# The root of one norm moved from the transposed rows into the values' copies and the means under the head norms

## The reference, cut to what matters

```python
h = h + sq_relu_mlp(rmsnorm(h, norm_mlp[0]), w_up[0], w_down[0])     # end of layer 0
kv = rmsnorm(h, kv_norm) @ w_kv                                      # (256, 512)
k_shared = rmsnorm(kv[..., :256].reshape(B, S, 4, 64), k_norm)       # norm of each head
v_shared = kv[..., 256:].reshape(B, S, 4, 64)
proj = rmsnorm(h, norm_mix[1]) @ w_in[1]                             # (256, 1024)
q = rmsnorm(proj[..., :768].reshape(B, S, 12, 64), q_norm)
mqh = rmsnorm(proj[..., 768:].reshape(B, S, 4, 64), mem_q_norm[1])
main_out = swa_sink_attention(q, k_shared, v_shared, sinks)
mem_out = memory_attention(mqh, mk, mv)
h = h + concatenate([main_out, mem_out]) @ w_out[1]
# rmsnorm(x, g) = x * rsqrt(mean(x * x) + 1e-6) * g
```

## Time and profile before

| | us |
|---|---|
| median of three executions | 1710.79 |
| lowest and highest | 1706.96, 1711.28 |
| profiled execution, first to last instruction | 1711.7 |
| the stretch from the last four matmuls of the down product to the first of `inb` | 1407.04 to 1430.55 |

### The profile page before, as it was taken

One profiled execution on the slowest core, in us unless ns is written; L12 is line 12 of the kernel. 1 busy time (PEld: TensorE's weight loads), 2 busy tenths in 40 slices (PEclk: granted clock), 3 DMA queues, 4 the chain that ended last, 5 costly groups with the idle time before them and its releaser, 6 DMA issues.

```text
span 1711.7 us, 19423 instructions
## 1 busy us (share of the span) xinstructions
PE 1510.8 (88%) x7216; PEld 1104.5 (65%) x7216; DVE 1124.4 (66%) x2042; ACT 749.0 (44%) x1378; POOL 274.8 (16%) x317
## 2 busy tenths in 40 slices
PE   7999999999997877777777777778999999899999
PEld 6899989988973332222223232238888879778887
DVE  6579665766576666666666776457576556757654
ACT  5544455443443333333333333235455346655532
POOL 0000000000023333333333433322000001100000
PEclk9999999999999999999999999999999999999999
DMA  6754434454489999999999999962355553125553
GB/s 232 260 185 164 158 133 150 171 173 130 169 331 420 420 421 421 421 421 421 422 409 413 423 414 421 418 264 91 114 207 183 191 191 130 50 83 212 179 192 121
DMA packets 71038, 442.02 MB, mean 258 GB/s; under 512 B 7031, under 2 KB 9343, under 8 KB 25504
## 3 DMA queue, kind: packets, MB, share of 16 engines
q0 software_dynamic: 36864, 268.45, 37.9%
q1 hardware_dynamic: 30208, 163.59, 27.9%
q10 hardware_dynamic: 3872, 8.75, 1.4%
HBM read 439.70 MB, written 2.63 MB: 258 GB/s over the span
## 4 chain that ended last, share of the span: by engine, by line
PE 62%; DMA 24%; DVE 8%; ACT 3%; issue 2%; POOL 0%; ACTq 0%; SPq 0%; DVEq 0%; POOLq 0%
DMA arena<-experts,xn 24%; PE banks L1159 18%; PE banks L1130 12%; PE banks L1190 11%; PE banks L1482 8%; PE banks L1195 6%; DVE arena L2057 2%; PE banks L1285 1%; DVE w_lo L1633 1%; PE banks L1237 1%; PE banks L1308 1%; ACT xn L928 1%; ACT xn L932 1%; ACT xn L921 1%; PE banks L1322 1%
## 5 line engine op out<-in xcount | busy, mean ns | idle before, releaser
L1482 PE MATMUL banks<-arena,xn 128*128 128x512 f32 x1024 | 484.4, 619 | 157.9 <-ACT xn L932 156.3
L1633 DVE TENSOR_TENSOR w_lo<-raw,w_hi 128x2048 fp32r<-128x2048 f32 x154 | 352.6, 2290 | 203.7 <-PE banks L1159 102.0
L1482 PEld LDWEIGHTS banks<-arena,xn 128*128 128x128 f32 x1024 | 189.6, 194 | 449.9 <-ACT xn L932 253.1
L2057 DVE CUSTOM_DVE_ANT_0 arena<-arena,banks 128x1024 f32<-128x1024 f32 x256 | 312.2, 1220 | 215.3 <-DMA arena<-experts,xn 215.3
L641 ACT ACTIVATE w_hi<-raw 128x2048 fp32r<-128x2048 f32 x154 | 295.1, 1918 | 248.7 <-PE banks L1159 128.8
L576 POOL DMA_INDIRECT arena<-experts,xn x256 | 243.1, 950 | 435.7 <-PE banks L1482 385.8
L1159 PE MATMUL banks<-w_hi,op 128*128 128x512 f32 x896 | 226.2, 392 | 0.0
L921 ACT ACTIVATE xn<-xn,stat 128x2 f32<-128x2 f32 x128 | 37.8, 295 | 396.9 <-DVE xn L2057 396.9
L1190 PE MATMUL banks<-op,w_hi 128*128 128x512 f32 x792 | 199.1, 393 | 0.0
L1159 PEld LDWEIGHTS banks<-w_hi,op 128*128 128x128 f32 x896 | 168.2, 189 | 35.1 <-issue 0.7
L1130 PE MATMUL banks<-op,w_hi 128*128 128x256 f32 x1376 | 187.7, 286 | 1.2 <-ACT op L666 1.2
(11 more groups left out here) (237 smaller groups left out, 1224.3 us busy)
## 6 DMA issues: line engine op xcount, KB each, us to landing
raw<-wstream SPq DMA_DIRECT2D x154, 1024.0 KB, 5.0
arena<-experts,xn POOLq DMA_INDIRECT x256, 13.3
xn<-mem_in ACTq DMA_DIRECT2D x2, 1024.0 KB, 7.1
scratch<-scratch ACTq DMA_DIRECT2D x1, 1536.0 KB
x<-x_in SPq DMA_DIRECT2D x2, 512.0 KB, 4.9
arena<-scratch ACTq DMA_DIRECT2D x1, 1024.0 KB, 8.0
arena<-keys_in ACTq DMA_DIRECT2D x1, 1024.0 KB, 4.9
out_dram<-x SPq DMA_DIRECT2D x4, 256.0 KB, 2.0
```

Source lines behind the costliest of these rows:

```text
L1482: mm = pe.matmul(sums[:, n, :], diag[:, s, :], rows[:, s, D + n * CW:D + (n + 1) * CW], start=(at == 0), stop=(at == PAIRS - 1), skip_grou ...
L1633: dve.tensor_tensor(w_lo[:, n % LO, :, :], raw[:, n % RAW, :, :], w_hi[:, n % HI, :, :].bitcast(F32), ALU.subtract).then_inc(lo_ready, 1)
L2057: dve.tensor_tensor_reduce(u, u, token_rows[k // PAIRS][:, :, :], 1.0, 0.0, ALU.mult, ALU.add, dots[:, s:s + 1]).then_inc(dot_ready, 1)
```

## The change

`mixb` takes the second form of the norm. Its rows, high and low, are those of x times the gain without the root r. Three things are done for it. The copies of the values take the scale r of each token, so two copies become four. The mean of each head's squares takes eps / r², which is eps times the mean square plus eps: for the keys TensorE adds it into `kr` by a matmul of `mean128` (all 1/128) with two diagonals that VectorE makes (`key_eps`), for the queries it is the bias of each token's root (`by_token`, `small[:, 0:2]`). VectorE makes `small` and the diagonals behind the low rows and in front of the memsets; ScalarE waits for the end of the down product before it writes buffer 0.

```diff
-ROOT_LATER = ("cross", "ffn", "mlpa", "mlpb")
+ROOT_LATER = ("cross", "ffn", "mlpa", "mixb", "mlpb")
...
-            def squares_and_rows(n, weight, buf):
+            def squares_and_rows(n, weight, buf, gain_=None):
...
-                    high_rows(n, n, buf, 0, range(2 * c, 2 * c + 2))
+                    high_rows(n, gain_ or n, buf, 0, range(2 * c, 2 * c + 2))
...
+                if key[0] == "qr":
+                    by_token(key, j, ACT.Sqrt)
+                    return
...
+            def by_token(key, j, f):
+
+                act.wait_ge(eps_ready, 1)
+                for tb in range(TB):
+                    c = slice(4 * tb, 4 * tb + 4)
+                    e = act.activation(query_root[:, j, c], misc_bank(key)[:, c], f, bias=small[:, tb:tb + 1])
+                empty_misc(e, key)
...
-            sum_squares_of_sum("mixb", "downa")
-            high_rows("mixb", "kv", 1, 0)
+            squares_and_rows("mixb", "downa", 1, "kv")
+            act.wait_ge(half_done, LAST[("downa", 3)])
             high_rows("mixb", "mixb", 0, 1)
...
-            for c in range(2):
-                e = act.activation(v_swa[:, :, :, c, c * HD:(c + 1) * HD], v[:, :, :, c, :], ACT.Copy)
+            for tb in range(TB):
+                for c in range(2):
+                    e = act.activation(v_swa[:, tb, :, c, c * HD:(c + 1) * HD], v[:, tb, :, c, :], ACT.Copy,
+                                       scale=roots_of("mixb")[:, tb:tb + 1])
...
-            roots(("kr",), sqk[:, 2:4, :])
+            wait_misc(act, ("kr",))
+            empty_misc(act.activation(sqk[:, 2:4, :], misc_bank(("kr",)).rearrange("p (a b) -> p a b", a=2), ACT.Sqrt),
+                       ("kr",))
...
-            mlp("a", product_and_norm(1, "outa", "mlpa", hi_made=mixed_a), "mixb")
-            keys_values(1, **normed("mixb", 0))
+            last_turns = mlp("a", product_and_norm(1, "outa", "mlpa", hi_made=mixed_a), "mixb")
+            half_chunk(True, 1, amid=last_turns, **normed("mixb", 0))
+            half_chunk(False, 1)
             pe.wait_ge(head_sq, 4)
             b = fill_misc(("kr",))
-            pe.matmul(b, mean64, sqk[:, 0:2, :], start=True, stop=True).then_inc(misc_full, 1)
+            pe.wait_ge(key_eps, TB)
+            pe.matmul(b, mean64, sqk[:, 0:2, :], start=True, stop=False, skip_group_check=True)
+            for c in range(2):
+                for tb in range(TB):
+                    at = c * S + tb * P
+                    mm = pe.matmul(b[:, at:at + P], mean128, root_diag[:, tb, :], start=False, stop=True,
+                                   skip_group_check=True)
+            mm.then_inc(misc_full, 1)
...
-            take_norm("mixb", [("kv", 1), ("mixb", 0)], [LAST[("downa", 3)] + 2] * 2)
+            add_and_take("downa", "mixb", "kv", 1, stats("mlpa")[1], last=False)
+            for j in range(4):
+                low_row("mixb", "mixb", 0, j, 1)
+            dve.tensor_scalar(small[:, 0:TB], stats("mixb")[2], 1e-6, None, ALU.mult).then_inc(eps_ready, 1)
+            dve.wait_ge(eps_ready, 1)
+            for tb in range(TB):
+                dve.tensor_scalar(root_diag[:, tb, :], ident, small[:, tb:tb + 1], float(P), ALU.mult, ALU.mult)\
+                   .then_inc(key_eps, 1)
             do(dve.memset(q_swa[HD:P, 0, :, :], 0.0))
```

More of the change, by code:

```diff
@@ L372, in build @@
         memory_roots = sem("memory_roots")
+        eps_ready = sem("eps_ready")
+        key_eps = sem("key_eps")
         swa_out = sem("swa_out")
@@ L690, in roots_of @@
                 return stats(n)[3]
-            def sum_squares_of_sum(n, weight):
-                for c in range(2):
[L695 to L701, removed]
             def exps(kind, u):
@@ L1055, in memory_means @@
             def memory_means():
[L1057 to L1060, removed]
+                wait_misc(act, ("qr", 3))
+                by_token(("qr", 3), 3, ACT.Identity)
             act.wait_ge(query_gains, 1)
@@ L1500, in mlp @@
                     if g == 3 and next_norm:
-                        product_and_norm((g + 1) % 2, "down" + l, next_norm, **split_made(f"hidden{l}{g}"), **k)
-                        continue
+                        return product_and_norm((g + 1) % 2, "down" + l, next_norm, **split_made(f"hidden{l}{g}"), **k)
                     tokens((g + 1) % 2, **split_made(f"hidden{l}{g}"), **k)
@@ L1711, in add_x, with add_and_take @@
                     add_piece(weight, j, times)
-            def add_and_take(weight, n, g, buf):
-                add_piece(weight, 0)
-                add_piece(weight, 1)
+            def add_and_take(weight, n, g, buf, times=None, last=True):
+                add_piece(weight, 0, times)
+                add_piece(weight, 1, times)
                 low_parts(LAST[(weight, 3)] + 1)
[L1718 to L1723, removed]
+                low_row(n, g, buf, 0, last=last)
+                low_row(n, g, buf, 1, last=last)
+                add_piece(weight, 2, times)
+                add_piece(weight, 3, times)
+                low_row(n, g, buf, 2, last=last)
+                low_row(n, g, buf, 3, last=last)
                 low_parts(LAST[(weight, 3)] + 2)
@@ L2227, in mlp @@
                     split(f"hidden{l}{g}", hidden[:, KC * g:KC * (g + 1), :], (g + 1) % 2)
-                add_x("down" + l, stats("mlp" + l)[1])
+                if l == "b":
+                    add_x("down" + l, stats("mlp" + l)[1])
             mlp("a")
-            take_norm("mixb", [("kv", 1), ("mixb", 0)], [LAST[("downa", 3)] + 2] * 2)
+            add_and_take("downa", "mixb", "kv", 1, stats("mlpa")[1], last=False)
[6 more added lines that the diff above has]
+                   .then_inc(key_eps, 1)
             do(dve.memset(q_swa[HD:P, 0, :, :], 0.0))
```

## The result

The changed kernel took 1713.88 us (median of ten runs, 1711.20 to 1715.01), the kernel before, in ten runs as well, 1707.47 (1706.48 to 1712.86). The ratio is 1.0028, 95% interval 1.0017 to 1.0038: 2.9 to 6.5 us slower, 4.8 by the ratio. (The medians differ by 6.4: the ten runs of before lie in two groups, near 1707 and near 1711, and their median lies in the lower one.) I had forecast +3.3 us, 1714.1 in all; that the absolute time fits to 0.2 us is partly luck, since the median of the three runs of before that I had lay 3.3 us above that of ten.

The account below looks back on a forecast made before the run. The chain of TensorE and the row gather bounds the kernel; TensorE would newly wait for VectorE's zeros. Zeros and copies +0.5, eight instructions +0.9, clock +1.9 make +3.3 us: median 1714.1 us, range 1707.5 to 1718.0.

Parts of the forecast that it names:

- T: Start of the norm's last transposes on TensorE, forecast at 1412.05 us by the timetable of the norm `ffn`.
- The step on which I settled: VectorE between norm and value copies: low rows until 1422.55, diagonals 0.65 us, zeros ready at 1428.6, 0.8 us later than before.
- Copies: ScalarE's value copies, two of 256 columns becoming four of 128 with a scale: +0.6 us on the path.
- Means: Start of the key means on TensorE: forecast at 1430.5 against 1429.99, +0.5 us from zeros and copies.
- Eight instructions: Four f32 matmuls added to the key means on TensorE: 0.9 us at full clock, 1.7 at half, all on the path.
- Clock: TensorE at half clock for 3.4 to 4.5 us after a 7.5 us idle time: 1.9 us lost, bounds 1.2 to 3.3.
- the third gap of the earlier trace: TensorE's 2.4 us idle time at 1463 to 1465.5, followed by more than 6 us near half clock in thinner work.
- the zeros are not the bound: Rival: VectorE reaches its memsets early, TensorE waits only for the copies; -4.3 us, 1706.5 us; chance 0.10.
- The gap costs no clock: Rival: TensorE's new idle time loses no clock, so the change costs +1.4 us, 1712.2 us; chance 0.15.
- The clock stays down long: Rival: half clock lasts as after 1465.5, or falls again elsewhere; +4.7 up to +7 us, about 1716.5; chance 0.20.
- The hidden parts: Moved squares, GpSimd's power, SyncE's weight loads and the queries' per-token roots (below 0.35 us), all claimed to cost nothing.
- the signs that I had named: Right: TensorE idle 6 to 8 us, half clock 3 to 5 us. Wrong: idle below 3 us, memsets before 1421.

Follow-up runs that it names:

- 1: Changed kernel with only the two small memsets of the values' buffer moved before the additions to x; timed +0.5 us against the kernel before.
- 2: Changed kernel with all four memsets moved early, between low weight parts of the down product; timed -4.4 us against the kernel before.
- 3: Control: the kernel before with the same early memsets, in front of the down product's `add_x`; timed +0.5 us (-1.4 to 2.4) against the kernel before.
- 4: Changed kernel with all four memsets early and the eps matmuls ahead of the wait for the squared keys; 1701.91 us, ratio 0.9963 to the kernel before.
- 8: Changed kernel with eight unused matmuls filling the idle time before the key means to size; timed +1.0 us against the kernel before.
- 5: Changed kernel with only the four eps matmuls moved ahead of the wait for the squared keys; timed +0.9 us against the kernel before.
- 9: Kernel before with three unused matmuls filling its 3.2 us idle time before the norm to size; timed -2.9 us against the kernel before.
- 7: Kernel before with six unused matmuls in its idle time before the norm, overfilling it; timed +0.2 us against the kernel before.
- 6: Changed kernel with fourteen unused matmuls between the values' half and the wait for the squared keys, overfilling the gap; timed +3.6 us against the kernel before.

## Why the prediction was right

The forecast (+3.3 us) and its case (the zeros hold the values, the clock falls) were right. By its own steps, with T the start of the last four transposes:

- *T*: 4.22 us after the last four down matmuls, as taken from `ffn` (1409.11 - 1404.89). The values' half starts at T + 4.78 (forecast 5.02; `ffn` had a wait of 0.2 us for a low row in it) and ends about T + 10.5 (10.8).
- *VectorE*: second gain's low rows from T + 6.24 to T + 10.18 (forecast 6.78 and 10.5), zeros done at 1425.43, T + 16.32 (16.55). The step on which I settled held within 0.3 us, with two errors in it that partly cancel: the rows started 0.54 us sooner and they and the memsets took 0.31 us longer. Experiments 1 and 2 against 3 show that it is the zeros and not another wait.
- *Copies*: 1.01 us to the next start against 0.55, +0.46 (forecast +0.6).
- *Means*: they start at 22.34 + 0.79 - 22.95 = +0.18 us against before (forecast +0.5): the zeros came 0.23 us sooner than forecast and the copies took 0.14 less, both to one side.
- *Eight instructions*: 0.90 us at full clock, by 4 against 2 (forecast 0.9).
- *Clock*: 2.83 us, by 8 and by 2 (forecast 1.9, bounds 1.2 to 3.3). This is the mis-sized term. I had taken the half stretch after a restart from the two gaps before dense work, 3.4 and 4.5 us; it was 6.1 us. The restart begins here with the means, ten small instructions, and the third gap of the earlier trace rows, with more than 6 us and thinner work behind it, was the nearer row. Experiment 5 speaks for this reading, since with two of the ten behind the gap the half stretch was 4.7 us, but its gap is shorter as well (5.80 us); what sets the length stays open.

Sum of the measured: 0.18 + 0.90 + 2.83 = +3.91 us, the stretch. The timed +4.8 holds this in its interval. Some 0.4 of the other 0.9 us lies behind the stretch, as the last section shows; what the rest is, if it is real, stays open.

Of the rivals, *the zeros are not the bound* was excluded by the trace; had they not been, 4.3 us would have been gained, and experiment 2, which takes them away, gained 4.58. *The gap costs no clock* would have been +1.4 and experiment 8, which makes it so, gives +1.08. *The clock stays down long* was priced at +4.7 or more with 3.3 for the clock; the stretch lies between it and the forecast, and the timed +4.8 alone could not have told the two apart. The hidden parts stayed hidden within the stretch: in 4 the zeros and the eps matmuls are moved and all else is as in the changed kernel, and the only waits of TensorE are those for high rows (0.94 us, as at `ffn`) and 0.63 us before and between the eps matmuls and the means.

Of the signs that I had named, the idle time (7.42 us, 6 to 8 forecast) and the transposes without a wait came true; half clock for 3 to 5 us did not (6.1). By the letter a sign of being wrong came too, memsets before 1421 (1420.63). But T is 1409.11 instead of 1412.05, because this profile is early as a whole: the memsets start at T + 11.52, against 11.15 in the forecast.

The page cited in the prediction (the Trainium skill, "TensorE: Matmul & The Clock Gate", Why this matters for your kernels, no idle gaps between bursts) is borne out by 8 and 9, 2.83 and 1.70 us, though not every gap costs: behind the 1.75 us before the means in 2 the granted clock stays 1.00. Of the three gaps that I gave there with 0.53 to 0.65, the row of the second has 0.78: it is the half microsecond in which the clock came back.

## What to carry to other kernels

When a wait is taken off the bounding engine, follow every other engine to what it must deliver next: here a memset with 1.0 us to spare became the bound when the values came 6.0 us earlier (the last eight matmuls of their half start 20.57 us after the last four down matmuls before, 13.80 + 0.79 now), and behind it stood a weight part as the next. Work that depends on nothing (zeros, constants, an eps term) belongs where its engine is idle, before the chain that the change shortens; for the zeros that is worth 0 us in the kernel before (3), but 8.5 us in the changed one (2). Two short idle times of the bounding engine merged into one long one are not a wash: price its restart too, here 2.83 us behind the long one against 1.70 behind the first of the short ones.

## What the runs showed of the hardware

Behind one short gap of this kernel the clock loss is not certain, but it is the same amount each time that it comes. All eleven profiles have the idle time of 2.4 us in the first steps of the attention (L1322, L1324 or L1326). In six of them (before, changed, 1, 3, 5, 7) half clock follows, in five (2, 4, 6, 8, 9) none, and the time from its end to the second product with the values is 8.16 to 8.20 us or 4.88 to 4.89. TensorE's timeline of the changed kernel, and of 8:

```profile
1466.41 0.55 PE L1326 MATMUL banks<-consts,arena 128*128 128x128 f32 x3 [2.41 <-DVE arena L1806]
...
1474.61 0.82 PE L1303 MATMUL banks<-arena 128*128 128x256 f32 x4
```

```profile
1463.04 0.55 PE L1326 MATMUL banks<-consts,arena 128*128 128x128 f32 x3 [2.41 <-DVE arena L1808]
...
1467.92 0.82 PE L1303 MATMUL banks<-arena 128*128 128x256 f32 x4
```

The instructions are the same, the idle time too; 3.3 us hang on it. That is nearly as much as the change costs. It is a good part of what scatters outside the stretch: there the six profiles with the loss take 1672.2 to 1676.3 us, the five without it 1668.9 to 1670.4. Each kernel has one profile, so whether the loss goes by the kernel or by the execution is not shown directly; but if before always had it and 2 never, 2 would be timed at 4.58 + 3.3 = 7.9 us less than before, and its interval ends at 6.0.

Something else goes by the kernel. All seven profiles with the new form of the norm, and none of the four without, have one more short wait late in the attention; TensorE's timeline of the changed kernel:

```profile
1491.88 0.55 PE L1326 MATMUL banks<-consts,arena 128*128 128x128 f32 x3 [0.33 <-DVE arena L1806]
```

From the end of the 2.4 us gap to the end of the span it is 246.2 to 246.3 us in the kernel before, 3 and 7, 246.6 to 246.7 in the changed one, 1 and 5, and, without the clock loss, 242.9 in 9 and 243.2 to 243.3 in 2, 4, 6 and 8. So the change costs some 0.4 us there that the prediction did not have; why is open.

Neither did I foresee the price of a float32 matmul of 512 columns: two instructions of 0.43 us each, 0.86 us at full clock. The Trainium skill ("FP8 and Floating Point Precision", TensorE Precision Notes) says that true float32 takes four passes through the array; the trace agrees: each of the two instructions takes 0.43 us, near twice the 0.23 us of a 512-column one in the rounded format (1404.89 to 1405.81 for four, in the changed kernel).
